# A hybrid attention and mLSTM step on one core: stream factors made ahead of the q and k norms, two weighings and the residual's scaled blocks moved

## The reference

```
z = rms_norm(x, g1) @ w_in             # q, k, v of attention; q, k, v, gates, output gate of the mLSTM
aq, ak = rms_norm(aq), rms_norm(ak)    # the q and k norms, per head and half, 128 wide
att = rms_norm((softmax(q1 k1) - lam * softmax(q2 k2)) v)
# mLSTM, 4 heads; for each stream a state C (256 x 128), n (128), m; gates ig, lf; block of 16 frames:
A   = exp(D - mt) * (q k^T)            # D from the gates; exp(D - mt) is the "expo" tile, the product the weighing
num = A v + iw * (C q),  den = sum(A) + iw * (n q),  h = num / max(|den|, exp(-mt))
sw  = exp(g - m_new)                   # a factor for each token and head
C_new = dec * C + sum_s sw v k^T,  n_new = dec * n + sum_s sw k
hm  = rms_norm(h) * sigmoid(mo)
x2  = x + concat(att, hm) @ w_out      # the residual stream
y   = x2 + square(relu(rms_norm(x2, g2) @ w_up)) @ w_down
```

## Time and profile before

| | |
|---|---|
| median of 3 runs | 1730.23 us (1728.5 to 1730.5) |
| the profiled execution, its own time | 1730.19 us |
| its span in the profile | 1728.4 us |
| PE busy | 1720.4 us, 100% |
| PEld busy | 1467.0 us, 85% |
| DVE busy | 906.1 us, 52% |
| ACT busy | 654.4 us, 38% |
| POOL busy | 405.2 us, 23% |
| granted clock | 1.00 over the whole span |

### The profile page before, as it was taken

One profiled execution on the slowest core, in us unless ns is written; L12 is line 12 of the kernel. 1 busy time (PEld: TensorE's weight loads), 2 busy tenths in 40 slices (PEclk: granted clock), 3 DMA queues, 4 the chain that ended last, 5 costly groups with the idle time before them and its releaser, 6 DMA issues.

```text
span 1728.4 us, 24600 instructions
## 1 busy us (share of the span) xinstructions
PE 1720.4 (100%) x8414; PEld 1467.0 (85%) x8414; DVE 906.1 (52%) x1669; ACT 654.4 (38%) x1224; POOL 405.2 (23%) x596
## 2 busy tenths in 40 slices
PE   9999999999999999999999999999999999999999
PEld 8999999999987888888888888887888888888887
DVE  5634776556687666545433554343465334456333
ACT  5324754444344444333332333232333332333332
POOL 2721010002451353433000343000343100234100
PEclk9999999999999999999999999999999999999999
DMA  7775479999998687665444565444556444556543
GB/s 191 204 170 151 127 173 213 218 207 216 250 256 260 155 219 204 177 186 159 125 131 122 166 184 175 130 125 124 160 166 182 141 130 122 164 165 171 173 144 97
DMA packets 295939, 295.18 MB, mean 171 GB/s; under 512 B 97184, under 2 KB 202716, under 8 KB 295836
## 3 DMA queue, kind: packets, MB, share of 16 engines
q1 hardware_dynamic: 255606, 222.91, 47.0%
q0 software_dynamic: 25168, 67.06, 14.8%
q10 hardware_dynamic: 15062, 3.86, 1.2%
HBM read 261.51 MB, written 38.02 MB: 173 GB/s over the span
## 4 chain that ended last, share of the span: by engine, by line
PE 97%; DVE 2%; issue 0%; DMA 0%; ACT 0%; ACTq 0%; DVEq 0%
PE bank L675 9%; PE bank L634 9%; PE bank L676 9%; PE bank L635 9%; PE bank L633 9%; PE bank L674 9%; PE acc L535 8%; PE acc L537 7%; PE acc L536 7%; PE bank L2075 3%; PE ssb L633 2%; PE ssb L634 2%; PE ssb L635 2%; PE ssb L674 2%; PE ssb L675 2%; PE ssb L676 2%
## 5 line engine op out<-in xcount | busy, mean ns | idle before, releaser
L515 DVE TENSOR_TENSOR w_lo<-raw,w_hi 128x512 fp32r<-128x512 f32 x768 | 537.9, 706 | 754.4 <-ACT w_hi L506 753.8
L506 ACT ACTIVATE w_hi<-raw 128x512 fp32r<-128x512 f32 x768 | 482.8, 631 | 958.5 <-PE acc L537 194.9
L535 PE MATMUL acc<-a_hi,w_hi 128*128 128x400 f32 (+1 forms) x768 | 267.6, 348 | 0.2 <-DVE w_lo L515 0.2
L536 PE MATMUL acc<-a_lo,w_hi 128*128 128x400 f32 (+1 forms) x768 | 263.1, 343 | 0.0
L537 PE MATMUL acc<-a_hi,w_lo 128*128 128x400 f32 (+1 forms) x768 | 262.6, 342 | 0.0
L614 POOL DMA_DIRECT2D u_turned<-m x192 | 123.8, 652 | 552.3 <-DVE m L2018 552.0
L675 PE MATMUL bank<-w_lo,a_hi 128*128 128x512 f32 x640 | 253.2, 396 | 0.0
L633 PE MATMUL bank<-w_hi,x2g_hi 128*128 128x512 f32 x640 | 252.2, 394 | 1.0 <-issue 1.0
L634 PE MATMUL bank<-w_lo,x2g_hi 128*128 128x512 f32 x640 | 253.0, 395 | 0.0
L676 PE MATMUL bank<-w_hi,a_lo 128*128 128x512 f32 x640 | 252.8, 395 | 0.0
L635 PE MATMUL bank<-w_hi,x2g_lo 128*128 128x512 f32 x640 | 252.5, 394 | 0.0
(11 more groups left out here) (351 smaller groups left out, 1819.8 us busy)
## 6 DMA issues: line engine op xcount, KB each, us to landing
raw<-in_w_up SPq DMA_DIRECT2D x128, 512.0 KB, 3.8
raw<-in_w_down SPq DMA_DIRECT2D x128, 512.0 KB, 3.8
raw<-in_w_in SPq DMA_DIRECT2D x94, 512.0 KB, 4.7
raw<-in_w_out SPq DMA_DIRECT2D x32, 512.0 KB, 5.4
u_turned<-m POOLq DMA_DIRECT2D x192, 64.0 KB, 2.9
stage<-u_turned POOLq DMA_DIRECT2D x16, 768.0 KB, 6.1
vc<-in_cache_v POOLq DMA_DIRECT2D x32, 256.0 KB, 7.3
kc<-in_cache_k SPq DMA_DIRECT2D x128, 64.0 KB, 3.6
```

The lines of the kernel that those rows point to most:

```text
L506: e.activation(w_hi[:, q], raw[:, slot, 4 * (q % 2):4 * (q % 2) + 4, :], ACT.Copy).then_inc(hi_ready, 1)
L515: e.tensor_tensor(w_lo[:, q], raw[:, slot, 4 * (q % 2):4 * (q % 2) + 4, :], w_hi[:, q].bitcast(F32), ALU.subtract).then_inc(lo_ready, 1)
L535: e.matmul(out, w_hi[:, q, kk], hi[:, k, at], start=k == 0, stop=False, skip_group_check=True)
L536: e.matmul(out, w_hi[:, q, kk], lo[:, k, at], start=False, stop=False, skip_group_check=True)
```

## The change

Three things are moved, and nothing is added to or taken from the arithmetic.

1. The four DMAs of `n_blk` and the one of `bmask` go from the end of attention to behind `row_cols` and `emcol`, under one semaphore `row_in` (12 DMAs). The transposition of `n_blk` and the ten instructions that make `bpair`, `swp` and `swm` go from `enter` to the place between DVE's loop over tiles 12 to 15 and `n_low(0)`. `enter` now waits for three DMAs.
2. `weigh` stands at offset 2 for all heads: heads 0 and 1 a quarter sooner, heads 2 and 3 as before.
3. `x2_due`: blocks 0 to 7 one to four quarters later, 8 and 9 one quarter later, 10 and 11 two, 12 to 15 one.

Six small tiles of SBUF become permanent for it, and `gmask` changes its place.

More of the change, by code:

```diff
@@ L124 @@
 OUT_STEPS = ("osum", "oroot", "oturn")
-HEAD_AT = (("rows", 0), ("decay", 0), ("scores", 1), ("expo", 1), ("ksw", 1), ("weigh", 3), ("cn", 4),
+HEAD_AT = (("rows", 0), ("decay", 0), ("scores", 1), ("expo", 1), ("ksw", 1), ("weigh", 2), ("cn", 4),
            ("take0", 4), ("take1", 5), ("take2", 5), ("take3", 6), ("num", 6), ("hsum", 6), ("cp", 7), ("og", 7),
@@ L365, in build @@
         gate_b = sb("gate_b", [NH, 2])
+        bmask = sb("bmask", [P, BD])
+        n_blk = sb("n_blk", [P, BD * NH])
+        nT = sb("nT", [P, BD, NH])
+        swm = sb("swm", [P, NH, BD])
+        bpair = sb("bpair", [P, 6])
+        swp = sb("swp", [P, NH, 2])
         with ExitStack() as s:
@@ L398, in build @@
             cB = sb("cB", [P, NH, TOK], scope=s)
-            gmask = sb("gmask", [P, 2, P], scope=s)
-            bmask = sb("bmask", [P, BD], scope=s)
-            n_blk = sb("n_blk", [P, BD * NH], scope=s)
             mo = sb("mo", [P, 2, 2, TOK], scope=s)
@@ L411, in build @@
             q_iw = sb("q_iw", [P, BD // 2, 2, 2 * TD], scope=s)
-            swm = sb("swm", [P, NH, BD], scope=s)
-            bpair = sb("bpair", [P, 6], scope=s)
-            swp = sb("swp", [P, NH, 2], scope=s)
+            gmask = sb("gmask", [P, 2, P], scope=s)
             k_swp = sb("k_swp", [P, 3, P], scope=s)
             C_pout = sb("C_pout", [P, DV // 32, 32], scope=s)
-            nT = sb("nT", [P, BD, NH], scope=s)
             n_new = sb("n_new", [P, 9, NH], scope=s)
@@ L818, in _ @@
                 for r in range(4):
-                    dma(row_cols[0:ROWS[r], r], gate_cols(2, 2 * NH, STARTS[r], ROWS[r]), "ml_in")
+                    dma(row_cols[0:ROWS[r], r], gate_cols(2, 2 * NH, STARTS[r], ROWS[r]), "row_in")
                 for x, at in enumerate((NPR, META, META + P)):
-                    dma(emcol[:, x], gate_cols(4, NH, at, P), "ml_in")
+                    dma(emcol[:, x], gate_cols(4, NH, at, P), "row_in")
+            for j in range(4):
+                dma(n_blk[32 * j:32 * j + 32], bass.AP(tensor=state_n.tensor, offset=32 * j, ap=[[DQ, BD * NH], [1, 32]]),
+                    "row_in")
+            dma(bmask[:], seq_of_row, "row_in")
             for n in range(16):
@@ L858, in _ @@
             done(e, ("o", STEPS[-1]))
-            for j in range(4):
-                dma(n_blk[32 * j:32 * j + 32], bass.AP(tensor=state_n.tensor, offset=32 * j, ap=[[DQ, BD * NH], [1, 32]]),
-                    "ml_in")
             dma(cB[:], bass.AP(tensor=gate_rows.tensor, offset=0, ap=[[0, P], [TOK, NH], [1, TOK]]), "ml_in")
             dma(gmask[:], gate_mask.rearrange("m p t -> p m t"), "ml_in")
-            dma(bmask[:], seq_of_row, "ml_in")
             dma(iwB[:], bass.AP(tensor=gate_rows.tensor, offset=NH * TOK, ap=[[0, P], [TOK, NH], [1, NS]]),
@@ L1881, in enter @@
             def enter():
-                e.wait_ge(S("ml_in"), 16 * 15)
+                e.wait_ge(S("ml_in"), 16 * 3)
                 done(e, ("o", STEPS[-1]))
-                e.transpose(nT[:].rearrange("p b h -> p (b h)"), n_blk[:]).then_inc(S("seq_paired"), 1)
                 e.memset(kv_rows[:, 3], 0.0).then_inc(S("pads_zero"), 1)
@@ L1892, in enter @@
                 e.memset(expo[:, EXPO_LATE:EXPO_LATE + P - META], 0.0)
[L1893 to L1901, removed]
             def head_work():
```

## The result

| | before | after |
|---|---|---|
| median (runs) | 1729.49 us (9: 1728.5 to 1730.81) | 1734.55 us (9: 1732.95 to 1735.11) |
| ratio, 95% interval | | 1.0026 [1.0018, 1.0034] |
| span of the profiled execution | 1728.4 us | 1731.1 us |

The change makes the kernel slower by 0.26% by the ratio (4.5 us); the medians lie 5.1 us apart. The interval leaves out 1, so the kernel is slower, by far less than 2%. A second measurement (experiment 5) gave 1.0033 [1.0021, 1.0045]. The forecast was 1730.0 us with a range up to 1731.9; the time lies outside.

The account below looks back on a forecast made before the run. PE bounds the kernel, busy 1720.4 of 1728.4 us. Gains of 0.61 (head 0) and 0.03 (head 1) against 0.45 lost at the norms make -0.19 us: from 1730.19 to 1730.0 us, range 1728.0 to 1731.9.

Parts of the forecast that it names:

- the sum: Whole kernel: -0.61 (head 0) - 0.03 (head 1) + 0.45 (norms) + 0 (DMAs) + 0 (residual) = -0.19 us.
- the last of its cases: A change no row foretells, such as an issue gap or tiles at new addresses: chance 0.08, half of it small.
- The rival that was to end slower: At the residual, turned rows land about 5 us later and PE waits for x2: 1733.7 us or more; chance 0.04.
- a stage without edits changes its length: Sign that the prediction is wrong, named beside PE showing a wait at the residual.
- The ends of the range: 1728.0 to 1731.9 us, from 1729.5 and 1730.6 widened by half the runs' spread and a 1 us issue gap.
- The weighing: Attention, head 0: weighing a quarter sooner cuts PE's step to cn from 0.89 to 0.28 us, gaining 0.61 us.
- The block in front of the norms: Moved instructions take 1.76 us of DVE against 1.3 us of cover, delaying n_lo; PE loses 0.45 us.
- The DMAs: n_blk's and bmask's five DMAs take 2.55 us of POOL's 2.94 us idle time; cost and gain zero.
- The residual: Later x2 blocks around tiles 61 to 67: nothing to gain, cost zero; up to 1 us if cover were gone.
- The two small terms: The weighing's gain (0.61 us in head 0, 0.03 in head 1) and the norms' loss of 0.45 us.
- The chance of 0.93: Whole kernel: chance that the time stays the same, beside 0.02 for faster and 0.05 for slower.
- PE's listed waits: Profile after: PE's listed waits together within 0.3 us of what they were, a sum below 5 us.

Follow-up runs that it names:

- experiment 5: The changed kernel measured again, on the same chip as the later runs: 1734.94 us, ratio 1.0033 to the kernel before.
- experiment 1: Kernel before with an unused 32-byte tile in front of x2g_hi, so x2g_hi and x2g_lo alone stand 32 bytes later: 1734.84 us, ratio 1.0030.
- experiment 2: Changed kernel with an unused 32-byte tile behind swp, putting all tiles behind it on multiples of 64 again: 1730.07 us, ratio 0.9996 to the kernel before.
- experiment 4: Kernel before with w_hi and w_lo alone 32 bytes later, a second unused tile bringing the rest back onto multiples of 64: 1737.03 us, ratio 1.0039.
- experiment 6: Kernel before with an unused 32-byte tile in front of w_hi, so w, a and x2g all stand 32 bytes off: 1729.62 us, ratio 1.0001.
- Experiment 9: Kernel before with the weighing of heads 0 and 1 a quarter sooner, nothing else: one run, 1733.0 us beside 1731.4 for the kernel before.
- experiment 8: Changed kernel with 32 unused bytes behind swp and the block of factors and normalisers one loop sooner on DVE: 1728.95 us, ratio 0.9999 to the kernel before.
- experiment 10: Like experiment 8, but with x2's blocks at their places of the kernel before: one run, 1730.18 us.
- experiment 7: Kernel before with a_hi and a_lo alone 32 bytes later, a second unused tile in front of y_rows: 1733.72 us, ratio 1.0025.

## Why the prediction was wrong

**The step that failed** is the sum's silence about where the tiles lie. The front of the document says that six small tiles become permanent; the prediction costed the DMAs and instructions that use them, and not what the tiles push. In the last of its cases it named "another step between weights of a kind that tiles at new addresses bring", gave all such things 0.08, and put half of that down as small. Its sum has no term for the up projection, and its range has no room for one. The missing term measured 1.9 ns for each of 2304 products, 4.4 us in all, some twenty-three times the size of the sum's -0.19 us. Its cause is not the address of `x2g` alone: the loaded `x2g` and the streamed `w` no longer start at the same remainder modulo 64 (experiments 1, 2, 4 and 6). One of the prediction's own signs of being wrong came true, "a stage without edits changes its length". The term could not be read from waits, since there are none, but it could have been asked: the tile with the most traffic in a stage of 530 us lay behind an edited list of tiles. The rival that was to end slower, x2's rows landing late, did not happen. The ends of the range do not follow from its own words either: half the spread of the runs and an issue gap of 1 us around 1729.5 and 1730.6 give 1727.5 to 1732.6, not 1728.0 to 1731.9. The time would have missed that range as well.

**What held, by the prediction's own steps:**
- *The weighing.* Forecast a step of 0.28 us in place of 0.89. Measured 453.50 - 453.24 = 0.26, with the last read of bank 3 ending at 452.08; forecast 451.8.

```profile
451.93 0.15 DVE L1821 TENSOR_TENSOR expo<-expo,bank 16x16 f32<-16x16 f32 x1
...
453.24 0.34 PE L535 MATMUL acc<-a_hi,w_lo 128*128 128x384 f32 x1
453.50 0.71 PE L2075 MATMUL bank<-k_sw,kv_rows 32*128 32x256 f32 x8
```

  The gain of 0.6 us is there, though one step towards it was too large. Of the 1.76 us taken out of `enter`, nearly all was to pass on, with the exponents at 448.5; they start at 449.05, 1.15 us sooner (1.3 against PE's products, which stand 0.15 us later there). A part of the rest shows in the trace: DVE now waits 0.16 us for ACT's split of weights in that stretch. The prediction didn't say whether the gain needs the lighter `enter`. Experiment 9 shows that it doesn't; without it the margin is 0.1 us.

```profile
444.69 0.69 DVE L513 TENSOR_TENSOR w_lo<-raw,w_hi 128x512 fp32r<-128x512 f32 x1 [0.16 <-ACT w_hi L504]
...
449.05 1.30 ACT L1268 ACTIVATE expo<-expo,row_cols 128x128 f32<-128x128 f32 x4 [2.29 <-DVE expo L1807]
```

- *The block in front of the norms.* Forecast 1.76 us of DVE and a loss of 0.45 us. Beside the earlier trace rows:

```profile
163.17 0.20 DVE L1607 STREAM_TRANSPOSE nT<-n_blk 128x32 f32<-128x32 f32 x1
...
164.93 0.96 DVE L1596 TENSOR_TENSOR n_lo<-n_sq,n_hi 128x768 fp32r<-128x768 f32 x1
...
165.34 0.34 PE L535 MATMUL acc<-a_hi,w_lo 128*128 128x400 f32 x1
...
166.00 0.19 PEld L2075 LDWEIGHTS ssb<-n_hi,ones_r 128*128 128x128 f32 x1 [0.65 <-issue]
166.03 0.41 PE L2075 MATMUL ssb<-n_hi,ones_r 128*128 128x384 f32 x1 [0.34 <-DVE n_lo L1596]
...
166.28 0.33 PE L2075 MATMUL ssb<-n_lo,ones_r 128*128 128x384 f32 x1
```

  164.93 - 163.17 = 1.76 us, to the hundredth. PE's step is 0.69 in place of 0.18, 0.51 us lost, and the step behind it is 0.25 in place of 0.17, so that PE stands 0.6 us later in all. The list of waits shows 0.3 of it only. The rest fits the load of weights: it starts 0.03 us ahead of its product here, and 0.18 us ahead of it in the kernel before (165.57 and 165.75). The product starts 0.14 us behind the end of `n_lo`, where the prediction took 0.05. The block cost PE nothing in experiment 8, one loop sooner, so its cost lies in its place. The Trainium skill's formula for operations between SBUF tiles ("VectorE: DVE Perf Modes", the TRN2 errata section) would have made the block an estimate of 0.75 us; the trace after disagrees with it as the one before did. The same section of the Trainium skill says that this formula comes out too low, and puts the measured fixed term at about 150 cycles. With that term the eleven instructions would be an estimate of 1.8 us, close to the 1.76 measured.
- *The DMAs.* On POOL, 2.04 and 0.55 us, and the first of `state_blocks` at 102.73: no cost, and DVE did not wait for `row_in`.

```profile
100.16 2.04 POOL L722 DMA_DIRECT2D n_blk<-in_state_n  x4
102.19 0.55 POOL L722 DMA_DIRECT2D bmask<-in_stream_mask  x1
102.73 1.10 POOL L722 DMA_DIRECT2D state_blocks<-in_state_C  x1
```

- *The residual.* Blocks 0 to 7 stand two or four quarters later, not one to four as the description of the change has it. ACT waited for landing rows for 2.1 us in two waits, where it had waited 7.0 us in three (two of them in the earlier trace rows); the forecast for those two was below 2. The statistics came later, the split of tile 65's q3 at 667.70 in place of 666.83, and PE took it at 670.66 without a wait. The cost is zero, as forecast, and experiment 10 bears it out.

```profile
ACT x2g_hi L1335 <- DMA m<-x_turned: 2.1, 2, 1.4
```
```profile
667.70 0.69 DVE L513 TENSOR_TENSOR w_lo<-raw,w_hi 128x512 fp32r<-128x512 f32 x1
```

The two small terms came out at -0.6 and +0.6 us, so that they cancel; the sum had -0.64 and +0.45. The chance of 0.93 for "no measurable change" was right for the mechanisms that were listed and far too high for the kernel. PE's listed waits came to 3.1 us together in place of 4.8, and not within 0.3 us of it as foretold, mostly because the issue gap of 1.0 us was absent.

**What stays open.** The up groups account for 4.4 us. The medians differ by 5.1 and 5.5 us in two measurements. Both intervals hold 4.4 us (3.1 to 5.9 us, and 3.6 to 7.8), and no stage of the profiles holds the rest. The issue gap alone was 1.4 us in one profile of the changed kernel and absent in the other, and 1.0 us before. The down groups are 0.07 us shorter each in both profiles of the changed kernel, which was not pursued. Also, x2g at 177056 costs 1.08 us a group and at 176608 only 0.92, with the same remainder modulo 64; why these differ was not tried. Why unequal remainders cost at all is not shown: no run looks inside a product. Only remainders 0 and 32 were tried. That tiles 0 to 47 hardly mind is measured, and not explained: their streamed operands have 384 or 400 columns, the roles of w and a are exchanged there, and the loaded and streamed operands stood differently in experiments 4 and 7.

## What to carry to other kernels

When an edit makes a tile permanent, drops one or changes a size, list the starts of all tiles before and after, and look at those that PE reads in the longest stage. Keep the loaded and the streamed operand of such a matmul on the same remainder modulo 64 bytes; here a padding tile of 32 bytes was enough. And where a kernel is slower with no new wait, compare steps from start to start, stage by stage: equal code with unequal steps points at data placement or clock, not at the schedule.

## What the runs showed of the hardware

- A float32r product of 512 columns steps by 231.5 to 231.9 ns on average when both SBUF operands start on the same remainder modulo 64 bytes (both 0, or both 32), and by 233.1 to 233.5 ns when one stands at 0 and the other at 32, whichever of them it is. With 384 or 400 streamed columns the difference is 0.3 ns at most (experiment 7), and nothing in sum when w was moved (experiment 4).
- The Trainium skill ("SBUF — State Buffer", on operand start alignment) asks for starts at multiples of the element size, which all tiles here keep. The Trainium skill says there that its rule is about what is legal, and not about speed; the runs add that keeping it is not enough for speed. The Trainium skill's matmul formula ("VectorE: DVE Perf Modes", the TRN2 errata section: 6 cycles and one for each column, at 2.4 GHz) gives an estimate of 216 ns for 512 columns; no group of such products here comes below 231 ns on average.
- The profile's own duration of the weight loads does not show the effect: the mean for the products with `x2g_hi` is 188 ns before and after. Before, then after:

```profile
L633 PEld LDWEIGHTS bank<-w_hi,x2g_hi 128*128 128x128 f32 x640 | 120.6, 188 | 29.0 <-issue 1.4
L631 PEld LDWEIGHTS bank<-w_hi,x2g_hi 128*128 128x128 f32 x640 | 120.3, 188 | 29.4 <-issue 0.4
```
